# Next layer's modulation weights in a two-layer diffusion backbone: issued without a wait for the pair rows

## The chip, the cores and the metric

The kernel runs on one core of a Trainium2 chip. The metric is the device time of one execution in microseconds (us), as the median of the runs. One core has five engines with instruction streams of their own: TensorE (PE in the profile; its weight loads are PEld), VectorE (DVE), ScalarE (ACT), GpSimd (POOL) and SyncE (SP). They meet only through semaphores. SP and POOL issue transfers, each into a queue of its own, and 16 DMA engines carry out both queues.

## The reference

Two layers (DEPTH = 2) of a hybrid backbone over 384 tokens of 1024 channels, 128 of them context and 256 latent. All data is float32.

```
for l in range(DEPTH):
    mod = silu(c) @ w_mod[l] + b_mod[l]          # 1024 -> 6 * 1024: shift, scale and gate, twice
    u = x * (1 + scale1) + shift1
    x = layer_norm(ALPHA * x + gate1 * token_mixer(u))
    u = x * (1 + scale2) + shift2
    x = layer_norm(ALPHA * x + gate2 * hier_moe(u))
```

`token_mixer` is one input projection (`w_in`), three head groups (pooling, differential attention, convolution) and one output projection (`w_out`). `hier_moe` sends each token to 2 of 32 gated experts and adds their two outputs with their weights:

```
h = silu(t @ w_gate[e]) * (t @ w_up[e])
y = sum over the token's two experts of  w[n, e] * (h @ w_down[e])
```

## The kernel before

Nothing of the weights stays on the core between layers: every weight is loaded from HBM once, in the order in which the layers use it. The big weights go through `ring`, four slots of 24 KB per partition (numbers 0 to 3), and during the experts through a fifth slot (number 4) that lies in `arena`. SP issues all of these loads in one order written out by hand. Before each it waits until the slot's last user is done, so a load that waits also holds back all that stands behind it in SP's stream.

A layer runs through these stages: modulation and input projection (`project`, PE line L828), attention and convolution, output projection (L1010), a first layer norm, the router, then 31 expert chunks `i` = 0 to 30 (between the 20th and the 21st of them some extra chunks for experts with more tokens), then the sum over each token's two experts, a second layer norm (`layer_norm(1)`, PE lines L988, L990 and L997) and, in the first layer, the modulation of the next one.

One chunk is: gather 64 token rows (POOL, L677), transpose them (PE, L1068), multiply by gate and up (PE, L1060), the gate (ACT, L1361, and DVE, L1790), multiply by down (PE, L1075; the last two chunks at L1084), copy out (ACT, L1386), and scatter the result rows to the HBM buffer `y_pairs` (POOL, L682). Chunks 29 and 30 scatter nothing: their results stay in `ystack` on the core. `down_done` counts the chunks whose down product PE has finished.

After chunk 28's scatter has landed, POOL reads `y_pairs` back as three blocks of 128 tokens (L751, into `yk`, 1 MB each, with 8 KB for one partition); each raises its `y_loaded`. These are the pair rows. DVE waits for each block, weighs its two halves and adds them (L1839, L1840), and raises `y_sum`. PE meanwhile multiplies the late chunks' results into place (L1165); then it waits for all three `y_sum` and adds the pair rows (L1174), eight tiles of 384 columns. DVE turns each tile into the residual (L1635, L1642) for the second layer norm.

The next layer's modulation weights come as three loads ("units", `load_mod` at L521, 3, 3 and 2 MB, again 8 KB for one row of one partition). Unit 0 goes into slot 2, whose last chunk is 27, unit 1 into slot 3 (chunk 28) and unit 2 into slot 1 (chunk 29). PE uses them in `mod_product` (L790): k = 0 and 1 inside the second layer norm, the rest after it. Behind the three units SP issues the next layer's `w_in` (L510), once chunk 30 is done.

Of the kernel before, what the change touches and what calls it, by code (L numbers as in the profile page):

```python
# [34 lines left out]
NT = T // P  # L35
# [148 lines left out]
def build(nc, g, consts, lam_dram, u_rows, y_pairs, y_prompt, y_sample, new_k, new_v):  # L184
    with ExitStack() as ctx:
# [3 lines left out]
        def signal(name, per_layer, step=1, credit=0):  # L189
            return Signal(ctx.enter_context(nc.semaphore(name)), per_layer, step, credit)  # L190
# [7 lines left out]
        arena = sb("arena", [P, 2 * XS])  # L198
        pool_sums = sb("pool_sums", [P, 4 * POOL_COLS])
        cst = sb("cst", [P, sum(n for _, n in CONST_COLS)])  # L200
        pool_blk = sb("pool_blk", [P, 2, P])
        conv_pw = sb("conv_pw", [P, 2, CONV])
# [245 lines left out]
        y_loaded = [signal(f"y_pairs_loaded{t}", 1, 16) for t in range(NT)]  # L448
# [8 lines left out]
        def engine_wait(eng):  # L457

            def wait(sig, l, n, alone=False):
                eng.wait_ge(sig.sem, sig.at(l, n))  # L460
                if alone:
                    eng.nop(nofuse=True)
            return wait
# [32 lines left out]
        def _(sp):  # L496
            wait = engine_wait(sp)
# [5 lines left out]
            for l in range(DEPTH):  # L503
# [13 lines left out]
                def load_mod(l_, j, u):  # L517

                    sp.nop(nofuse=True)
                    k0_, k1_ = MOD_K * u, min(KD, MOD_K * (u + 1))  # L520
                    sp.dma_start(mod_w[MOD_SLOTS[j][u]][:, 0:k1_ - k0_, :],  # L521
                                 w_mod[l_:l_ + 1, k0_ * P:k1_ * P, MOD_STEP * j:MOD_STEP * (j + 1)].rearrange(
                                     "o (k p) n -> p (o k) n", p=P)).then_inc(mod_loaded[u].sem, 16)
# [91 lines left out]
                    load_chunk(i)  # L615

                if l + 1 < DEPTH:
                    for t in range(NT):
                        wait(y_loaded[t], l, 1)
                    for u in range(3):  # L620
                        wait(down_done, l, max(i for i in range(NS) if SLOT_OF[i] == MOD_SLOTS[0][u]) + 1)
                        load_mod(l + 1, 0, u)
# [1256 lines left out]
```

## Time and profile before

| | us |
|---|---|
| median of 3 runs | 1119.69 (1119.44 to 1121.03) |
| profiled execution, device time | 1117.82 |
| its span, first to last instruction | 1116.0 |
| PE busy | 929.8 |
| DMA engines, mean rate over the span | 288 GB/s |

All views below are of that one profiled execution; times are us from the start of its span. A row of a timeline is: start, duration, engine, line, operation, destination<-sources, count, and in brackets the engine's idle time before it with what ended it. A row of the chain of work that ended last is: start, duration, engine and line. A row of waits is: who <- whom: us in total, times, longest. A queue's row has its packets, its MB and its share of the 16 DMA engines' time in that stretch: q1 is SP's queue, q0 is POOL's. A row of stretches gives the stretch, its length, busy us of PE, PEld, DVE, ACT and POOL (with instructions), then the granted TensorE clock (1.00 is 2.4 GHz, 0.50 is 1.2 GHz), the DMA engines' busy share and their GB/s. SPq is SP's sequencer as it issues a transfer. A line can be that of a helper.

### The profile page before, as it was taken

The page shows a single profiled execution, that of the slowest core. Times are in us where ns is not written, and L with a number is a line of the kernel's source. Part 1 is how long each engine was busy: PE and PEld are TensorE (multiplying, and loading weights), DVE is VectorE, ACT ScalarE, POOL GpSimd, SP SyncE. Part 2 cuts the span into 40 slices and gives each one's busy share as a digit, 9 for nine tenths or more (in the row PEclk, how much of TensorE's full clock was granted, in tenths as well). Part 3 has the DMA queues.
Part 4 walks back from the last instruction along what each step waited for, and adds up shares of the span by engine and source line. Part 5 has one row for each costly group of instructions (what it writes and reads, how often), then busy time and mean ns, then how long its engine had stood idle before and what let it go on. Part 6 is the DMA issues. An engine that isn't in the chain of part 4 may idle for free.

```text
span 1116.0 us, 13925 instructions
## 1 busy us (share of the span) xinstructions
PE 929.8 (83%) x5252; PEld 549.2 (49%) x5252; DVE 382.8 (34%) x921; ACT 236.9 (21%) x565; POOL 180.0 (16%) x217
## 2 busy tenths in 40 slices
PE   4899988994999877898899989898598896888872
PEld 2456555543555534454455546554355553444441
DVE  0258463255111111113537855126411111111162
ACT  1200166033111100111220036406011110111122
POOL 5000000003223322221020000000333222222100
PEclk8899989996999998999899999999699999989996
DMA  9972163177999999997994226038699999999811
GB/s 359 380 299 77 44 235 154 52 303 288 357 412 415 414 413 413 410 386 278 401 346 182 113 95 268 34 129 345 234 399 413 415 415 383 398 411 411 344 58 57
DMA packets 73136, 321.88 MB, mean 288 GB/s; under 512 B 13150, under 2 KB 17590, under 8 KB 48752
## 3 DMA queue, kind: packets, MB, share of 16 engines
q1 hardware_dynamic: 57824, 294.14, 66.2%
q0 software_dynamic: 15248, 26.87, 6.6%
q8 instruction: 42, 0.69, 0.3%
q14 instruction: 22, 0.18, 0.0%
HBM read 321.46 MB, written 23.59 MB: 309 GB/s over the span
## 4 chain that ended last, share of the span: by engine, by line
PE 62%; DMA 15%; DVE 9%; SPq 8%; ACT 3%; issue 3%; POOLq 0%; POOL 0%; DVEq 0%; ACTq 0%
PE ps L828 13%; PE ps L1060 13%; DMA ring<-in_w_up 9%; PE ps L1010 7%; PE ps L1075 7%; PE ps L831 4%; DMA ring<-in_w_in 3%; SPq L559 3%; SPq L566 2%; SPq L561 2%; PE ps L790 2%; PE ps L997 2%; PE ps L1068 2%; DMA arena<-u_rows,row_idx 1%; PE ps L1084 1%
## 5 line engine op out<-in xcount | busy, mean ns | idle before, releaser
L1060 PE MATMUL ps<-ring,tail 128*64 128x256 f32 x1760 | 204.4, 383 | 12.4 <-DMA ring<-in_w_up 10.6
L1060 PEld LDWEIGHTS ps<-ring,tail 128*64 128x64 f32 x1760 | 143.9, 138 | 84.9 <-issue 24.4
L828 PE MATMUL ps<-uT,ring 128*128 128x384 f32 x448 | 149.7, 492 | 4.1 <-DMA ring<-in_w_in 2.1
L1790 DVE TENSOR_TENSOR arena<-arena,ps 128x128 f32<-128x128 f32 x68 | 19.5, 287 | 364.7 <-ACT arena L1361 364.7
L828 PEld LDWEIGHTS ps<-uT,ring 128*128 128x128 f32 x448 | 85.5, 192 | 60.7 <-issue 3.7
L1075 PE MATMUL ps<-ring,krow 128*64 128x512 f32 x408 | 103.5, 626 | 3.0 <-issue 2.1
L682 POOL DMA_INDIRECT y_pairs<-tail,row_idx x58 | 57.6, 994 | 291.3 <-ACT tail L1386 279.8
L677 POOL DMA_INDIRECT arena<-u_rows,row_idx x66 | 68.9, 1043 | 38.0 <-issue 20.1
L1386 ACT ACTIVATE tail<-ps 128x512 f32<-128x512 f32 x58 | 34.6, 597 | 189.5 <-PE ps L1075 189.5
L1508 DVE SCALAR_TENSOR_TENSOR arena<-arena,dw 128x414 f32<-128x414 f32 x118 | 67.6, 643 | 0.0
L1361 ACT ACTIVATE arena<-ps 128x128 f32<-128x128 f32 x68 | 18.8, 277 | 214.8 <-PE ps L1060 198.6
L1010 PE MATMUL ps<-arena,ring 128*128 128x384 f32 x192 | 62.2, 486 | 0.0
L1068 PE MATMUL ps<-cst,arena 128*128 128x128 f32 x272 | 42.3, 285 | 21.2 <-DMA arena<-u_rows,row_idx 17.4
L1785 DVE COPY tail<-ps 128x512 f32<-128x512 f32 x68 | 46.6, 691 | 37.1 <-PE ps L1068 29.6
L790 PE MATMUL ps<-ring,sT 128*32 128x512 f32 (+1 forms) x512 | 51.7, 544 | 6.2 <-DMA ring<-in_w_mod 6.2
L1122 PE MATMUL ps<-cst,arena 128*128 128x128 f32 x62 | 20.4, 328 | 42.9 <-DVE arena L1790 42.9
L1635 DVE SCALAR_TENSOR_TENSOR uT<-ps,modT,uT 128x128 f32<-128x128 f32 x64 | 23.5, 411 | 81.7 <-PE ps L1010 74.6
L1075 PEld LDWEIGHTS ps<-ring,krow 128*64 128x64 f32 x408 | 29.7, 140 | 41.2 <-issue 41.2
L1010 PEld LDWEIGHTS ps<-arena,ring 128*128 128x128 f32 x192 | 36.5, 190 | 25.4
L1060 PE MATMUL ps<-arena,tail 128*64 128x256 f32 x416 | 48.2, 383 | 0.0
L1068 PEld LDWEIGHTS ps<-cst,arena 128*128 128x128 f32 x272 | 32.2, 146 | 26.4 <-issue 21.0
L1060 PEld LDWEIGHTS ps<-arena,tail 128*64 128x64 f32 x416 | 36.2, 139 | 15.7 <-issue 7.5
(269 smaller groups left out, 980.1 us busy)
## 6 DMA issues: line engine op xcount, KB each, us to landing
ring<-in_w_gate SPq DMA_DIRECT2D x55, 1024.0 KB, 17.8
ring<-in_w_up SPq DMA_DIRECT2D x55, 1024.0 KB, 22.6
ring<-in_w_down SPq DMA_DIRECT2D x55, 1024.0 KB, 23.6
ring<-in_w_mod SPq DMA_DIRECT2D x12, 3072.0 KB, 11.2
arena<-in_w_gate SPq DMA_DIRECT2D x13, 1024.0 KB, 15.8
arena<-in_w_up SPq DMA_DIRECT2D x13, 1024.0 KB, 19.3
arena<-in_w_down SPq DMA_DIRECT2D x13, 1024.0 KB, 18.9
ring<-in_w_mod SPq DMA_DIRECT2D x6, 2048.0 KB, 15.9
```

What stands on the lines that cost most here:

```text
L677: pool.indirect_dma_start(xg[:, b, :], None, u_rows, bass.IndirectOffsetOnAxis(ap=idx, axis=0), bounds_check=2 * T - 1, oob_is_err=False). ...
L682: pool.indirect_dma_start(y_pairs, bass.IndirectOffsetOnAxis(ap=idx, axis=0), rows, None, bounds_check=4 * T - 1, oob_is_err=False).then_i ...
L790: last = mm(ps[32 * g_:32 * (g_ + 1), bank, 0:n], sT[:, 2 * k:2 * k + 32], mod_w[MOD_SLOTS[j][u]][:, row, off + g_ * n:off + (g_ + 1) * n] ...
L828: last = mm(ps[:, n % 4, 0:T], slot[s][:, k, c:c + P], uT[:, k, :], start=(k == 0), stop=(k == KD - 1))
L831: last = mm(ps[:, n % 4, 0:AW], uT[:, k, rows * P:(rows + 1) * P], slot[s][:, k, c:c + AW], start=(k == 0), stop=(k == KD - 1))
L1010: last = mm(ps[:, m % 4, 0:T], wt, mixT[:, k, :], start=(k == 0), stop=(k == KD - 1))
L1060: last = mm(ps[W * half:W * (half + 1), b, 0:2 * P].rearrange("p (j f) -> p j f", j=2), xc[:, b, k, :], gate_up_w[s][:, :, k, half * P:(ha ...
L1068: last = tr(ps[:, 5 + b, c * P:(c + 1) * P], xg[:, buf, c * P:(c + 1) * P], ident)
L1075: last = mm(ps[W * half:W * (half + 1), 3 + b, :], hT[:, b, f * W:(f + 1) * W], down_w[s][:, f, half * 512:(half + 1) * 512], start=(f == ...
L1386: fn(yrow[:, i % 2, :], ps[:, 3 + i % 2, :], ID).then_inc(y_rows.sem, 1)
L1508: conv_own.append(own.add(v.scalar_tensor_tensor(cacc[:, c, :], src, wt, cacc[:, c, :], ALU.mult, ALU.add)))
L1785: v.tensor_copy(xc[:, b].rearrange("p (h j) n -> p j h n", h=2), ps[:, 5 + b, :].rearrange("p (j h n) -> p j h n", j=4, h=2)).then_inc(sig ...
```

## The change

SP no longer waits for the three blocks of pair rows before it issues the three units of the next layer's modulation weights. The wait of each unit for its own slot stays.

```
                 if l + 1 < DEPTH:
-                    for t in range(NT):
-                        wait(y_loaded[t], l, 1)
                     for u in range(3):
                         wait(down_done, l, max(i for i in range(NS) if SLOT_OF[i] == MOD_SLOTS[0][u]) + 1)
                         load_mod(l + 1, 0, u)
```

SP's stream at the end of the first layer, in one piece of the difference: the last expert load (L566), the three units (L521, `ring<-in_w_mod`), and the read of a table that opens the next layer. In brackets stand the semaphores that an instruction waits for; `y_pairs_loaded0` to `2` are `y_loaded`.

```order
 L561 DMA ring<-in_w_up 128x2048
 L566 DMA ring<-in_w_down 128x2x1024 [waits down_done]
-L521 DMA ring<-in_w_mod 128x3x2048 [waits down_done,y_pairs_loaded2,y_pairs_loaded0,y_pairs_loaded1]
-L521 DMA ring<-in_w_mod 128x3x2048 [waits down_done]
+L521 DMA ring<-in_w_mod 128x3x2048 [waits down_done] x2
 L521 DMA ring<-in_w_mod 128x2x2048 [waits down_done]
 L467 TENSOR_LOAD turns_tab
```

No instruction moves within a stream, and the other engines' streams are the same; only the three semaphores ahead of unit 0 are gone.

## Rows read from the trace of the kernel before

**Rows 1.** The profile page: span, and the chain that ended last, by engine.

```profile
span 1116.0 us, 13925 instructions
...
PE 62%; DMA 15%; DVE 9%; SPq 8%; ACT 3%; issue 3%; POOLq 0%; POOL 0%; DVEq 0%; ACTq 0%
```

**Rows 2.** The chain that ended last, end of the first layer.

```profile
522.84 3.63 PE ps L1084 x8
526.49 1.03 ACT arena L1379
527.56 5.43 PE ps L1165 x16
532.99 2.69 PE ps L1174 x24
```

**Rows 3.** SP's waits, 495 to 610 us.

```profile
SPq L460 <- DMA arena<-y_pairs: 28.9, 1, 28.9
```

**Rows 4.** Timeline of SP's issues, 495 to 600 us.

```profile
527.47 1.44 SPq L521 DMA_DIRECT2D ring<-in_w_mod  x3
529.59 32.51 SPq L510 DMA_DIRECT2D ring<-in_w_in  x7
```

**Rows 5.** Timeline of PE, 499 to 550 us.

```profile
500.62 1.94 PE L1075 MATMUL ps<-ring,krow 128*64 128x512 f32 x8
...
507.46 1.94 PE L1075 MATMUL ps<-ring,krow 128*64 128x512 f32 x8
...
517.33 0.59 PE L1084 MATMUL ps<-ring,krow 128*64 128x512 f32 x1
...
532.83 5.52 PE L1174 MATMUL ps<-cst,arena 128*128 128x128 f32 x48
542.06 1.65 PE L988 MATMUL ps<-arena,cst 128*128 128x384 f32 x2 [3.71 <-DVE arena L1642]
```

**Rows 6.** Timeline of PE, 540 to 566 us.

```profile
544.92 3.02 PE L790 MATMUL ps<-ring,sT 128*32 128x512 f32 x16
547.87 5.43 PE L997 MATMUL ps<-arena,cst 128*128 128x384 f32 x16
553.22 5.36 PE L790 MATMUL ps<-ring,sT 128*32 128x512 f32 x48
...
561.97 4.43 PE L828 MATMUL ps<-uT,ring 128*128 128x384 f32 x13 [2.02 <-ACT uT L1211]
```

**Rows 7.** Timeline of POOL, 497 to 521 us.

```profile
510.85 0.97 POOL L682 DMA_INDIRECT y_pairs<-tail,row_idx  x1 [5.82 <-DMA y_pairs<-tail,row_idx]
517.35 1.68 POOL L751 DMA_DIRECT2D arena<-y_pairs  x3 [5.53 <-DMA y_pairs<-tail,row_idx]
```

**Rows 8.** Line L751, 500 to 530 us: issue to landing of its three loads.

```profile
DMA to landing us min/median/max: 5.0/6.9/8.9
```

**Rows 9.** Line L682, 1040 to 1049 us: the last two scatters of the second layer.

```profile
DMA to landing us min/median/max: 6.4/6.5/6.5
```

**Rows 10.** Timeline of DVE, 521 to 545 us.

```profile
527.37 0.75 DVE L1839 TENSOR_SCALAR arena<-arena,r 128x1024 f32<-128x1024 f32 x1 [0.41 <-DMA arena<-y_pairs]
528.15 1.28 DVE L1840 SCALAR_TENSOR_TENSOR arena<-arena,r 128x1024 f32<-128x1024 f32 x1
533.80 1.39 DVE L1635 SCALAR_TENSOR_TENSOR uT<-ps,modT,uT 128x128 f32<-128x128 f32 x4 [4.36 <-PE ps L1174]
```

**Rows 11.** DMA queues, 520 to 526 us: the pair rows alone.

```profile
q0 software_dynamic: 345, 2.56, 101.2%
```

**Rows 12.** DMA queues, 508 to 518 us: the last expert weights.

```profile
q1 hardware_dynamic: 361, 1.73, 42.0%
q0 software_dynamic: 160, 0.07, 2.6%
```

**Rows 13.** DMA queues, 18 to 24 us: both queues full, start of the kernel.

```profile
q1 hardware_dynamic: 208, 1.70, 70.5%
q0 software_dynamic: 215, 0.72, 30.6%
```

**Rows 14.** Stretches of 5 us with clock and DMA, around the second layer norm.

```profile
535.00:540.00 5.00, 3.35 (x30) 3.16 (x29) 4.86 (x13) 0.00 (x0) 0.00 (x0) 1.00 1.00 421
540.00:545.00 5.00, 2.94 (x8) 1.25 (x12) 2.60 (x7) 0.00 (x0) 0.00 (x0) 0.53 1.02 426
```

More of the change, by code:

```diff
@@ L617, in _ @@
                 if l + 1 < DEPTH:
-                    for t in range(NT):
-                        wait(y_loaded[t], l, 1)
                     for u in range(3):
```

## The prediction

> **What bounds the kernel now.** I read the page first, then the chain of work that ended last, then the streams of SP, PE, POOL and DVE around the one place that the change touches, 500 to 562 us. Over the whole span the chain is mostly PE [rows 1], so the question is what PE waits for there. At the end of the first layer the chain runs through PE and ACT without a hole: the down product of chunk 30, ACT's copy, the products of the late chunks (L1165) from 527.56, then the sum of the pair rows (L1174) at 532.99, in the instant at which L1165 ends [rows 2]. So the pair rows are not what PE waits for: DVE finished the third block's sum at 528.15 + 1.28 = 529.43 [rows 10], and 532.99 - 529.43 = **3.56 us** of slack lie between.
>
> Nor are the modulation weights waited for. SP stood 28.9 us before it issued them [rows 3], at 527.47 [rows 4], yet L790 follows its predecessor on PE with no idle time at 544.92 and at 553.22, and the first product of the next layer (L828) waits 2.02 us for ACT's uT and not for `w_in` [rows 6]. SP's 28.9 us are the wait of an engine that nobody is waiting for.
>
> **The change part by part.** *Removed:* the three waits on `y_loaded`. Unit 0 then needs only chunk 27's down product, which ends at 500.62 + 1.94 = 502.56; unit 1 chunk 28's, at 507.46 + 1.94 = 509.40; unit 2 chunk 29's, at 517.33 + 0.59 = 517.92 [rows 5]. Against 527.47 they are issued 25, 18 and 9.5 us earlier. What that gains on the chain is **0**, since no PE instruction of these stages waits for them. `w_in`, next in SP's stream, then waits for chunk 30 alone, 522.84 + 3.63 = 526.47 [rows 2], and goes out 529.59 - 526.47 = 3.1 us earlier: also 0, as L828 waits for ACT.
>
> *Moved:* 8 MB of weights (8.39 million bytes) now meet the pair rows in the DMA engines. Behind chunk 30's expert weights in SP's own queue they delay none of these, so the experts keep their times. POOL's queue is the other one. How much of the 8.39 MB is still to come when the pair rows are issued at 517.35 [rows 7]? From 508 to 518 the engines moved 1.73 + 0.07 = 1.80 MB [rows 12]; at the full rate, 2.56 MB in 6 us = 427 GB/s [rows 11], they could have moved 4.27 MB. The room is 2.5 MB, so at least 5.9 MB of modulation weights are still queued or just being issued: more than the 3.15 MB of the three blocks. The two queues compete for the whole length of the pair rows.
>
> How they share is seen where both were full before: from 18 to 24 us, 208 packets of q1 against 215 of q0 [rows 13]. They take turns packet by packet. Pair rows and modulation rows are both moved as 8 KB pieces, so each queue gets half the bytes. Alone, the pair rows take 3.15 MB / 427 GB/s = 7.4 us; at half the rate 14.7 us. The third block, which landed at 527.37 (where DVE's wait for it ends [rows 10]; 8.9 us after its issue [rows 8]), would land **7.4 us later, at 534.8**. DVE needs 0.75 + 1.28 = 2.03 us for it: `y_sum` at 536.8. PE is through with L1165 at 532.99. The sum: 7.4 - 3.56 = **+3.8 us** of new idle time on PE ahead of L1174. What hid the pair rows before was L1165 and chunk 30; that cover is used up after 3.56 us. Bounds: 0 if the pair rows lost under half of the 7.4 us, +3.8 if they share throughout.
>
> *The scatter ahead of them.* The pair rows are issued when chunk 28's scatter, issued at 510.85, has landed, 6.5 us later [rows 7]. It too now meets weights. At the end of the second layer, with expert weights still coming, the same scatters landed after 6.4 and 6.5 us [rows 9], so I put 0, between 0 and +0.3.
>
> *PE's clock.* A hole of 3.71 us ahead of L988 goes with a granted clock of 0.53 in 540 to 545 us [rows 5, 14], so half the time and more at 1.2 GHz. The new hole is about as long and may bring such a stretch over L1174. Its 48 instructions take 5.52 us, 0.69 us for each of eight tiles; at 1.2 GHz 1.38 us. DVE, which turns the tiles into the residual, starts at 533.80 [rows 10] and lets L988 go after seven of them at 542.06, 1.2 us for each, so it sets the pace and only the first tile is paid in full: **+0.7 us**, from 0 to +1.0. The stretch that now lies on L988 to L790 may move: 16 matmuls of L790 took 3.02 us at 544.92, where 48 took 5.36 us at 553.22 [rows 6], so 16 cost 1.2 us more; with half of L988's 1.65 us and as much for L990, which also lie in it, I bound the gain at 2.8 us. If the stretch fell on L997 instead, up to half of its 5.43 us again, +2.7 us. I take 0 for it, as both are open.
>
> *Queued behind.* All that follows is tied to PE in order: the next layer's `mod_product`, `w_in` of slot 1 (it waits for `mod_rows`), and then the second layer, where each slot is freed by PE. I see no place where 4 us would be won back; a delay here arrives at the end whole.
>
> The sum is 3.8 + 0 + 0.7 = +4.5 us: on the profiled execution 1117.8 + 4.5 = 1122.3, on the median, 1.9 us above it, **1124.2 us** (+0.4%).
>
> **The rivals.** *The pair rows stay hidden.* If the weights got less than half of the engines while the pair rows move, the loss stays under 3.56 us and nothing is left of the change: **1119.7 us**. For it: the slack is real, and the kernel has idle DMA time at 508 to 518. Against it: that room holds 2.5 of 8.4 MB, and turns were equal in rows 13. That unit 0 does not go out early, since something else in SP's stream holds it, would end here too; I see nothing that would. Together 0.15.
>
> *The clock moves to the good side.* The place is L988 to L790. If the stretch at 1.2 GHz falls on the new hole and on L1174, where DVE sets the pace, then L988, L990 and L790 run at 2.4 GHz and win up to 2.8 us: with a hole of next to nothing 1119.7 - 2.8 = **1116.9**. It decides at a hole of 2.8 us, above which it wins nothing; my sum has 3.8. 0.04.
>
> *The weights take more than every second turn.* If q1 drained several 8 KB pieces for each piece of q0, the pair rows would come last: (5.9 + 3.15) MB / 427 GB/s = 21 us from about 518.7, `y_sum` at 542, hole 9 us, **1129 to 1132 us**. Rows 13 speak against it (208 to 215). 0.04. The Trainium skill's page "DMA: Bandwidth & Descriptors" (section "Queues, rings and completion order") has such a rule: an engine goes round the queues, but drains a whole packet, typically 9 to 17 descriptors, before it turns to the next. By that with one piece for one descriptor the time would be this rival's; the trace so far shows equal turns of what it records as packets, and no row here shows how many descriptors one holds.
>
> **How the numbers follow.** Forecast 0.77, hidden 0.15, clock 0.04, unequal turns 0.04. The forecast's own range is from 3.8 - 2.8 = +1.0 (the clock at its best) to 3.8 + 0.3 + 1.0 + 2.7 = +7.8 (scatter and clock at their worst): 1120.7 to 1127.5. Leaving the hidden case out would leave out over 2 in 10, so the range goes down to it: 1119.5 to 1127.5. A measurement can tell about 0.2%, 2.2 us, from no change. Slower by more: all of unequal turns and nearly all of the forecast, 0.79; within: the hidden case and the forecast's low end, 0.17; faster: 0.04.
>
> **What would show it.** In the changed kernel's profile: L521 issued near 502.6, 509.5 and 518 us; in the 8 us after the pair rows' issue, q0 and q1 with about as many packets each; a third landing of some 16 us for L751 where it was 8.9; PE idle some 4 us ahead of L1174, ended by DVE's L1840, where it had no idle time; the granted clock below 1.00 in that stretch; and the second layer shifted as a whole by the same 4 to 5 us. L751's third landing under 12 us would make the sum wrong at its main term; a hole of 4 us with an unchanged total would mean that the loss is won back in the second layer, where I see no place for it.

## The result, and the profile after

| | before, us | changed, us | ratio, 95% interval |
|---|---|---|---|
| first comparison (4 runs each) | 1120.13 | 1129.95 (1128.75 to 1133.26) | 1.0079 (1.0056 to 1.0102) |
| second comparison (26 and 6 runs) | 1121.79 (1117.71 to 1127.56) | 1131.96 (1127.10 to 1133.74) | 1.0083 (1.0054 to 1.0112) |

The change makes the kernel slower by about 0.8%, 9 us (the ratios are estimated from all runs and are not the quotients of the two medians). The forecast was slower by 4.5 us, and the time lies above its range of 1119.5 to 1127.5 us. It lies within the 1129 to 1132 us of the rival of unequal turns; the packets below show that this is chance. The sign and the place were right; the size was half.

The profiled execution of the changed kernel took 1133.26 us, its span is 1131.2 us. Lines of the changed kernel stand two below those of before (L1174 is now L1172, L1165 is L1163, L751 is L749). SP's issues, answering to [rows 4]:

```profile
504.40 15.72 SPq L521 DMA_DIRECT2D ring<-in_w_mod  x3
528.30 19.64 SPq L510 DMA_DIRECT2D ring<-in_w_in  x3
```

The three units go out from 504.40 on (this execution is 1.8 us late at that point, a drift out of the start of the kernel: its product for chunk 27 ends at 504.33 instead of 502.56). The chain of work that ended last no longer runs through PE here, as it did in [rows 2]:

```profile
512.62 7.16 DMA y_pairs<-tail,row_idx
519.85 0.52 issue
520.37 0.86 POOL arena L749 x2
521.49 18.61 DMA arena<-y_pairs
540.12 0.76 DVE arena L1837
540.91 1.29 DVE arena L1838
542.25 2.94 PE ps L1172 x12
```

It goes through the scatter, POOL's issue of the pair rows, 18.61 us for the third block to land (8.9 in [rows 8]), DVE's sum, and only then PE. PE's timeline, answering to [rows 5, 6]:

```profile
529.33 5.43 PE L1163 MATMUL ps<-arena 128*128 128x384 f32 x16 [1.11 <-ACT arena L1377]
542.25 7.07 PE L1172 MATMUL ps<-cst,arena 128*128 128x128 f32 x48 [7.49 <-DVE arena L1838]
552.90 1.65 PE L986 MATMUL ps<-arena,cst 128*128 128x384 f32 x2 [3.58 <-DVE arena L1640]
...
573.29 2.26 PE L826 MATMUL ps<-uT,ring 128*128 128x384 f32 x3 [2.02 <-ACT uT L1209]
```

PE now stands idle for 7.49 us ahead of L1172 until DVE's L1838, where it had no idle time. From the start of L1163 (L1165) to the first L826 (L828) of the second layer PE needs 573.29 - 529.33 = 43.96 us; before it was 561.97 - 527.56 = 34.41 [rows 2, 6]. That is **+9.55 us**: 7.65 from the start of L1163 to that of L1172 (12.92 instead of 5.27), 1.42 from there to L986, 0.48 to L826. The rest of this profile's difference is 1.8 us from the start of the kernel, 3.1 us at L826 itself (below, at the third profile) and 0.8 us in attention.

Why the third block lands so late is told by the packets of the two queues, answering to [rows 11, 13]. From POOL's issue to 524 us, then 524 to 534 us:

```profile
q1 hardware_dynamic: 185, 1.50, 100.0%
```

```profile
q1 hardware_dynamic: 276, 2.13, 51.1%
q0 software_dynamic: 272, 2.10, 50.4%
```

For 3.6 us after its issue no pair row moves at all: 185 weight packets do. From then on the two queues take equal turns, as forecast.

### The profile page after: what moved, and what is told of

Read it like the earlier page. It is cut to its first block, busy times and chain, and to the rows that moved or that the text cites. A ratio compares the mean times of both kernels' runs of the same rounds, so it can differ in the third digit from the quotient of the medians.

```text
span 1131.2 us, 13924 instructions
## 1 busy us (share of the span) xinstructions
PE 933.2 (82%) x5252; PEld 551.5 (49%) x5252; DVE 383.3 (34%) x921; ACT 237.5 (21%) x565; POOL 180.1 (16%) x217
## 4 chain that ended last, share of the span: by engine, by line
PE 60%; DMA 16%; SPq 8%; DVE 8%; ACT 3%; issue 3%; POOL 0%; POOLq 0%; DVEq 0%; ACTq 0%
PE ps L826 13%; PE ps L1058 12%; DMA ring<-in_w_up 9%; PE ps L1008 7%; PE ps L1073 7%; PE ps L829 4%; SPq L559 3%; DMA ring<-in_w_mod 3%; SPq L561 2%; PE ps L788 2%; SPq L566 2%; PE ps L995 2%; DMA y_pairs<-tail,row_idx 2%; DMA arena<-y_pairs 2%; PE ps L1066 2%
## 5 line engine op out<-in xcount | busy, mean ns | idle before, releaser
L826 PE MATMUL ps<-uT,ring 128*128 128x384 f32 x448 | 152.7, 499 | 3.7 <-ACT uT L1209 3.7
L826 PEld LDWEIGHTS ps<-uT,ring 128*128 128x128 f32 x448 | 87.0, 195 | 61.8 <-issue 7.7
L788 PE MATMUL ps<-ring,sT 128*32 128x512 f32 (+1 forms) x512 | 51.4, 542 | 9.1 <-DMA ring<-in_w_mod 9.1
```

The source lines that it names most:

```text
L788: last = mm(ps[32 * g_:32 * (g_ + 1), bank, 0:n], sT[:, 2 * k:2 * k + 32], mod_w[MOD_SLOTS[j][u]][:, row, off + g_ * n:off + (g_ + 1) * n] ...
L826: last = mm(ps[:, n % 4, 0:T], slot[s][:, k, c:c + P], uT[:, k, :], start=(k == 0), stop=(k == KD - 1))
```

## The experiments

All hold the rest of the kernel as it is; r4_small_pieces, r6_pieces_4k and r8_small_rows also raise the semaphore counts that go with more loads. Ratios are to runs of the kernel before on the same chip (median 1121.79 for r1 to r4, 1121.08 for r5 to r8). The third landing counts from the issue of the last load of the pair rows.

| run | what differs from the changed kernel | median, us | ratio, 95% interval | third landing, us | PE idle ahead of the sum, us |
|---|---|---|---|---|---|
| before | the wait on the pair rows | 1120.13 | | 8.9 | 0 |
| changed | | 1129.95 | 1.0079 (1.0056 to 1.0102) | 18.6 | 7.49 |
| r1_again | nothing | 1131.96 | 1.0083 (1.0054 to 1.0112) | 18.7 | 7.65 |
| r2_after_scatter | units wait for the scatters | 1128.72 | 1.0064 (1.0040 to 1.0089) | 18.8 | 6.38 |
| r3_unit0_early | units 1 and 2 wait as before | 1123.32 | 1.0020 (1.0001 to 1.0038) | 15.0 | 3.15 |
| r4_small_pieces | weights in 2 KB pieces | 1121.10 | 0.9997 (0.9973 to 1.0020) | 13.0 | 0.74 |
| r5_again | nothing, one run | 1127.26 | | 18.7 | 7.80 |
| r6_pieces_4k | weights in 4 KB pieces | 1122.87 | 1.0024 (1.0006 to 1.0042) | 14.9 | 2.67 |
| r7_after_block0 | units wait for the first block | 1121.43 | 1.0005 (0.9991 to 1.0018) | 10.1 | 0 |
| r8_small_rows | pair rows in 2 KB pieces | 1138.14 | 1.0157 (1.0129 to 1.0186) | 23.1 | 16.69 |

**The changed kernel again (r1_again).** No edit.

> The changed kernel once more, for its spread and a second profile. The first profile has a hole of 7.5 us on PE ahead of the sum of the pair rows (forecast 3.8), 2.1 us more up to the first L826 of the second layer, and there 3.1 us more in a stretch at 1.2 GHz. Theory A (the hole is made by queues and repeats, the clock stretch over L826 does not): a hole of 7 to 8 us again; a device time near 1129 us if L826's 64 instructions take 20.9 us as before, near 1132 us if they take 23.9 us. Theory B (the size of the hole is itself chance): a hole that differs by over 2 us from 7.5 us.

The hole is 7.65 us and the third landing 18.7 us after its issue: the hole repeats, as in theory A. Its profiled execution took 1132.54 us and has 23.89 us for L826's first 64 instructions; among its runs are also 1127.10 and 1128.35.

**Units behind the scatters (r2_after_scatter).**

```
                 if l + 1 < DEPTH:
+                    for b in range(2):
+                        wait(y_stored[b], l, (PUT + 1 - b) // 2)
                     for u in range(3):
```

> SP waits for the landing of the last scatters, as POOL does, so the three modulation units are issued in the same instant as the pair rows, with nothing of them queued ahead. Theory A (the 3.7 us over the forecast come from weights that were already queued in the DMA engines: 1.25 us on the scatter, 2.3 us before the first pair row moves; the equal turns cost the forecast 7.4 us): scatter back at 6.5 us, third landing of L749 16 to 17 us after its issue (18.6 in the changed kernel), hole near 3.8 us, device time 1124 to 1126 us. Theory B (POOL's transfers start late whenever weights move, whoever was first): third landing 18 to 19 us, hole 6 us, 1127 to 1128 us.

SP and POOL now issue within half a microsecond of each other. SP, POOL and PE in the timeline:

```profile
517.86 1.61 SPq L521 DMA_DIRECT2D ring<-in_w_mod  x3
```

```profile
511.97 0.97 POOL L682 DMA_INDIRECT y_pairs<-tail,row_idx  x1 [5.83 <-DMA y_pairs<-tail,row_idx]
518.37 1.68 POOL L751 DMA_DIRECT2D arena<-y_pairs  x3 [5.43 <-DMA y_pairs<-tail,row_idx]
```

```profile
540.48 7.51 PE L1174 MATMUL ps<-cst,arena 128*128 128x128 f32 x48 [6.38 <-DVE arena L1840]
```

From the scatter's issue to that of the pair rows it is 518.37 - 511.97 = 6.40 us, where the changed kernel has 7.75 (520.37 - 512.62) and the one before 6.50 [rows 7]. So the weights queued ahead cost the scatter 1.3 us, and the hole falls by 1.1 us with it (the ratio of 1.0064 cannot be told from the changed kernel's). But the third block still lands after 18.8 us, and the hole of 6.4 us is theory B's number. My theory A fell on this point: a long line of weights ahead is not needed for the late start. The packets between POOL's issue and 522.3 us are all weights:

```profile
q1 hardware_dynamic: 167, 1.27, 90.6%
```

The half microsecond by which SP is first is enough.

**Unit 0 alone early (r3_unit0_early).**

```
                     for u in range(3):
+                        if u == 1:
+                            for t in range(NT):
+                                wait(y_loaded[t], l, 1)
                         wait(down_done, l, ...)
```

> Only unit 0 goes out early; units 1 and 2 wait for the pair rows as before. Seen over all engines, unit 0's 3.15 MB nearly fit into the 2.5 MB of room that the DMA engines had between 508 and 518 us. Theory A (the room is not spread evenly: the engines that finish the last expert weights late, at 518 us, have all of unit 0 still to move, and a block of pair rows lands with its slowest engine): third landing 14 to 18 us, hole 2 to 7 us, device time 1122 to 1129 us. Theory B (room is room): at most 0.7 MB of unit 0 is left, third landing near 11 us, no hole, 1119.5 to 1121 us.

Unit 0 by itself makes a hole of 3.15 us. It also costs the scatter 1.0 us: from its issue at 513.46 to that of the pair rows at 520.97 it is 7.51 us, where it was 6.50. DVE's three blocks:

```profile
530.34 0.75 DVE L1840 TENSOR_SCALAR arena<-arena,r 128x1024 f32<-128x1024 f32 x1 [4.49 <-DMA arena<-y_pairs]
...
534.66 0.75 DVE L1840 TENSOR_SCALAR arena<-arena,r 128x1024 f32<-128x1024 f32 x1 [2.24 <-DMA arena<-y_pairs]
...
537.12 0.75 DVE L1840 TENSOR_SCALAR arena<-arena,r 128x1024 f32<-128x1024 f32 x1 [0.40 <-DMA arena<-y_pairs]
```

The second block comes 4.3 us after the first, the third 2.5 us after the second, which is the pace of pair rows alone (7.4 us for three). From 522 to 524 us and from 524 to 530 us the packets are:

```profile
q0 software_dynamic: 40, 0.33, 48.6%
q1 hardware_dynamic: 39, 0.32, 37.9%
```

```profile
q0 software_dynamic: 291, 2.16, 85.6%
q1 hardware_dynamic: 47, 0.35, 14.1%
```

With equal turns on all 16 engines the weights would go on at half of the time until they run out on all of them together. Instead they keep on at 14% of it for 6 us. The packets don't name their engine, but this reads as most engines having no weights left after 524 us and a few still having some, and the block lands with these. The numbers are theory A's: the room of 2.5 MB between 508 and 518 us [rows 12] is not shared evenly by the engines, and an average over 16 of them hides it. Pair rows also begin to move 1.3 us after their issue (13 packets of q0 from 522.2 to 523.2, with the issue at 520.97), as in the kernel before; the weights took 38.9% of the engines' time between that issue and 522.2. So POOL's transfers are not late in themselves. They start late where the engines are full of weights.

**Weights in 2 KB pieces (r4_small_pieces).**

```
+                    n = MOD_STEP // pieces
+                    for c in range(pieces):
+                        sp.dma_start(mod_w[...][:, 0:k1_ - k0_, c * n:(c + 1) * n], w_mod[... + c * n ...])
...
-                        load_mod(l + 1, 0, u)
+                        load_mod(l + 1, 0, u, 4)
```

> The three units go out as early as in the changed kernel, but each as four loads of 512 columns, so in pieces of 2 KB instead of 8 KB. Theory A (turns are taken piece by piece, whatever its size, and the start of the pair rows waits for a number of pieces): an 8 KB pair row of 309 ns now alternates with 88 ns, so the pair rows take 9.5 us instead of 14.7 us, and start some 0.6 us instead of 2.3 us late: third landing 11.5 to 13 us, hole 0 to 1 us, 1119.5 to 1121.5 us. Theory B (the queues share by bytes or time): third landing 16 to 19 us and a hole of 4 to 7.5 us, 1125 to 1130 us.

The units go out as early as in the changed kernel, the total is that of the kernel before, and the hole is 0.74 us. The packets from 524 to 530 us:

```profile
q0 software_dynamic: 265, 1.93, 78.8%
q1 hardware_dynamic: 257, 0.52, 22.7%
```

Still one packet each, 265 to 257, but the pair rows now take 1.93 MB against 0.52. The late start was mis-sized here: pair rows are absent from their issue at 519.68 to 522.1 (2.4 us, against 1.3 us in the kernel before and 3.6 in the changed one), so it is 1.1 us and more, and not the quarter of 2.3 us that I had expected.

This run also answers whether the early units cost anything outside the pair rows. To within the interval, about 0.25% either way, they do not: with the pair rows less disturbed and a hole of 0.74 us, the loss is gone.

**The changed kernel a third time (r5_again).** No edit.

> The changed kernel a third time, for a profile. Two profiles had L826 of the second layer with a stretch at 1.2 GHz (23.9 us for its first 64 instructions instead of 20.9) and device times of 1133.3 and 1132.5 us; other runs of it took 1127 to 1129 us. Theory A (that stretch is the difference between the two): a device time near 1129 us comes with 20.9 us for L826, one near 1132 us with 23.9 us; the hole ahead of L1172 is 7.5 us in either. Theory B (the hole itself differs): a fast run with a hole of 4 to 5 us.

One run, with a device time of 1127.26 us and a hole of 7.80 us, so theory B falls. PE's timeline:

```profile
543.50 8.58 PE L1172 MATMUL ps<-cst,arena 128*128 128x128 f32 x48 [7.80 <-DVE arena L1838]
554.23 0.91 PE L986 MATMUL ps<-arena,cst 128*128 128x384 f32 x2 [2.15 <-DVE arena L1640]
...
571.69 20.88 PE L826 MATMUL ps<-uT,ring 128*128 128x384 f32 x64 [2.02 <-ACT uT L1209]
```

L826 takes 20.88 us as before, where the first two profiles have 23.93 and 23.89. The granted clock at that place, first the profile of the result, then this one:

```profile
573.00:578.00 5.00, 4.71 (x8) 2.62 (x9) 4.62 (x15) 4.26 (x9) 4.26 (x8) 0.50 1.04 416
```

```profile
571.00:576.00 5.00, 4.31 (x14) 2.62 (x15) 4.66 (x13) 4.66 (x10) 3.86 (x7) 1.00 1.03 414
```

In one the engine is at 1.2 GHz, in the other at 2.4. PE had the same gap of 2.02 us ahead of L826 in both. Here also L986 and L788 ran at 2.4 GHz (0.91 us for two where the first profile has 1.65), so from L986 to L826 it took 17.46 us instead of 20.39. The clock thus makes about 6 us of difference between two profiled executions with nearly the same hole, of which theory A had the half at L826. That is about the spread of all runs, 1127 to 1134 us; the others have no profile.

**Weights in 4 KB pieces (r6_pieces_4k).** The edit of r4_small_pieces, with 2 for 4.

> The units as early as in the changed kernel, each as two loads of 1024 columns, in pieces of 4 KB, between the 8 KB of the changed kernel and the 2 KB of the former run. Theory A (turns piece by piece): a pair row of 309 ns alternates with 159 ns, 11.2 us for all instead of 14.7 and 9.5; with a late start of 1.3 to 2 us the third landing is 14 to 15 us after its issue, the hole 1.5 to 3 us, the ratio to before 1.002 to 1.005. Theory B (2 KB pieces were harmless for another reason, such as their longer issue on SP): a hole under 0.8 us or one as long as in the changed kernel.

Third landing 14.9 us, hole 2.67 us, ratio 1.0024: all three within theory A. Equal turns again from 524 to 530 us:

```profile
q0 software_dynamic: 220, 1.67, 66.9%
q1 hardware_dynamic: 216, 0.86, 35.6%
```

The late start is as long as with 8 KB pieces: no pair row moves from the issue at 518.83 to 522.6, 3.8 us. That is 2.5 us more than in the kernel before, where theory A had put 1.3 to 2.

**Units behind the first block (r7_after_block0).**

```
+                    wait(y_loaded[0], l, 1)
                     for u in range(3):
```

> SP waits for the first block of the pair rows alone, then issues the units as their slots allow. Theory A (what counts is who is in the engines first, and how long the two are there together): at that landing some 2 of 3 blocks are through, the rest alternates, third landing at most 12 us after its issue, no hole, ratio 1.000. Theory B (pair rows are slowed whenever weights are issued near them): third landing 14 us or more and a hole of 2 us or more.

Third landing 10.1 us, no idle time on PE, ratio 1.0005. Pair rows that are in the engines first lose 1.2 us to the weights that come 5 us behind them, and 3.56 us of slack cover it.

**Pair rows in 2 KB pieces (r8_small_rows).** The reverse of r4_small_pieces, to double the suspected cost.

```
-                    pool.dma_start(yk[:, t, :], ...)
+                    for r_ in range(4):
+                        pool.dma_start(yk[:, t, r_ * 512:(r_ + 1) * 512], ...)
```

> The changed kernel with the pair rows in pieces of 2 KB (four loads for each block) and the weights in 8 KB as before: the reverse of the run with small weight pieces. Theory A (turns piece by piece): 96 small pair rows for each engine stand against 8 KB weight rows first and 2 KB rows of w_in later, 19 us for the first half and 8 us for the second, third landing some 27 to 30 us after the first issue, hole 15 to 18 us, device time 1138 to 1143 us. Theory B (shares by bytes or time): a hole of 8 to 9.5 us, 1129 to 1134 us.

```profile
550.46 7.56 PE L1173 MATMUL ps<-cst,arena 128*128 128x128 f32 x48 [16.69 <-DVE arena L1839]
```

```profile
q1 hardware_dynamic: 387, 2.80, 68.7%
q0 software_dynamic: 385, 1.27, 32.4%
```

The hole is 16.69 us. From 524 to 534 us the queues move 387 and 385 packets, and the pair rows get under a third of the bytes. A share by bytes or by time would have given 8 to 9.5 us by the estimate of theory B. The landing's 23.1 us count from the last of twelve issues, which POOL spreads over 6.5 us; from the first it is 29.0, within theory A's 27 to 30.

But what took turns was not what theory A had added up. The packets by size in the same 10 us:

```profile
DMA packets 772, 4.07 MB, mean 407 GB/s; under 512 B 98, under 2 KB 98, under 8 KB 438
```

The mean packet of q0 is 1.27 MB / 385 = 3.3 KB, more than a piece. Over the whole transfer the trace has 768 packets of 4096 bytes, two of the 2 KB pieces in each, and 16 packets of 4 bytes for each of the twelve loads. The equal counts include the small ones. So an engine had on average 48 packets of pair rows and not 96, and that the hole came out within 15 to 18 us is in part luck. The run shows equal turns by packet; it does not show them piece by piece.

## Why the prediction was wrong in size

**What bounds, and what the change gains.** Right. The 3.56 us of slack, nothing gained on PE, no instruction of PE waiting for the modulation weights: r4_small_pieces and r7_after_block0 have the units early and are as fast as the kernel before, not faster.

**The turns.** Right in packets, and shown at three sizes of weight pieces and with small pair rows. The Trainium skill's page "DMA: Bandwidth & Descriptors" (section "Queues, rings and completion order") says that an engine goes round its queues packet by packet. The trace agrees for what it records as packets, 276 to 272, 265 to 257 and 387 to 385. The rival of unequal turns is refuted by these counts, though its 1129 to 1132 us were met: its 9 us of hole came from pair rows that move last, and the measured 7.5 us do not. How many pieces one packet holds is another matter: with 8 KB rows it is one, in r8_small_rows it is two.

**The step that failed: what the pair rows and the scatter lose before the first turn.** The working put the whole loss into the 7.4 us of shared turns and let them start as soon after the issue as before (1.3 us). Measured, the third landing is 18.6 - 8.9 = 9.7 us later: 7.4 of turns, and 2.3 of a late start (3.6 against 1.3) that the sum did not have. The scatter, put at 0 to 0.3 us by [rows 9], lost 1.25 us (7.75 against 6.50). The sum then comes out: 1.25 + 2.3 + 7.4 - 3.56 = 7.4 us, where the profile has 7.49 and the forecast 3.8.

Both could be read in the trace of before. The 6.5 us of [rows 7] run from the scatter's issue to the issue of the pair rows, the 6.4 and 6.5 us of [rows 9] from issue to landing, so the working set two different measures side by side. From issue to landing chunk 28's scatter took 5.9 us, while the weights took 38.9% of the engines' time from its issue to 512.4 us. The first scatter of [rows 9] was issued at 1039.68 with the engines full of expert weights, and nothing of it moves for 4.1 us. Before, 510.85 to 512.4 us, then 512.4 to 513.4, then 1039.68 to 1043.8:

```profile
q1 hardware_dynamic: 34, 0.25, 38.9%
...
y_pairs<-tail,row_idx POOLq DMA_INDIRECT x1, 5.9
```

```profile
q0 software_dynamic: 50, 0.00, 2.5%
```

```profile
q1 hardware_dynamic: 321, 1.72, 102.5%
...
y_pairs<-tail,row_idx POOLq DMA_INDIRECT x1, 6.4
```

So [rows 9] did show a loss, of 0.5 to 0.6 us; in the changed kernel it is 1.25 us (7.16 in the chain above, against 5.9). Why it is larger there stays open.

The late start comes with engines that are busy with weights (r3_unit0_early), needs no long queue ahead (r2_after_scatter), and falls away when the pair rows are there first (r7_after_block0). What sets its length stays open. Beyond the 1.3 us of before it is 2.3 us or more with 8 KB pieces, 2.5 with 4 KB and 1.1 with 2 KB. With the 309, 159 and 88 ns for a piece that the expectations use, that is by estimate about 7, 16 and 13 pieces for each engine, or 60, 64 and 25 KB: neither one number of pieces, nor one amount of data, nor one time fits all three.

**The average over engines.** The 2.5 MB of room were an average. The forecast came to full sharing all the same, since 5.9 MB were left; but with unit 0 alone the same working would have said that nearly nothing is left, and r3_unit0_early measures a hole of 3.15 us.

**The clock.** L1172 to L986 took 1.42 us more where I had put 0.7, at most 1.0 (L1172's first 12 products took 2.94 us, where 24 took 2.69 [rows 2]). The rival of the good side did happen, in r5_again, at the place and nearly with the price that I gave (L986 to L826 2.4 us shorter than the 19.91 us of before, against 2.8), but beside a hole of 7.8 us. What I had not seen is a stretch at 1.2 GHz over L826, 3.1 us, in two of the three profiles. It is part of the spread from 1127 to 1134 us. The hole of 7.5 us alone would have left the forecast's +4.5 too low, by 3 us, but within its range (1119.7 + 7.5 = 1127.2). In the profiled execution the clock's 1.42, 0.48 and 3.1 us come on top; r5_again, where it gave back 2.4 us, took 1127.26 us.

**The second layer.** Right: from L826 on the delay arrives whole. From the first L826 to the end of the span it is 1125.4 - 571.69 = 553.7 us in r5_again, where it was 1116.0 - 561.97 = 554.0 before.

## What to carry to other kernels

A wait of an idle queue engine can be worth its time: it kept a load that nobody needed yet out of the way of one that had 3.56 us to spare. Before bringing a bulk load forward, look at what the other queue moves in that stretch: count its packets and not its bytes, add a late start on top of the shared turns, and take the slowest engine and not the mean. Where both must move at once, put the urgent transfer in first, or cut the other one into smaller pieces.

## What the runs showed of the hardware

- Two queues that both have work on the DMA engines move equal numbers of packets, whatever the sizes: 276 to 272 at 8 KB each, 257 of 2 KB to 265 of 8 KB, 216 of 4 KB to 220 of 8 KB, and 387, most of 8 KB, to 385, most of 4 KB (small packets counted). The size of a packet is thus a priority.
- A packet is not always one piece: POOL's 2 KB rows moved two to a packet of 4 KB (r8_small_rows, mean 3.3 KB), SP's 2 KB rows one to a packet (r4_small_pieces, 0.52 MB / 257 = 2.0 KB).
- A transfer of POOL's that comes to engines full of SP's 4 or 8 KB pieces starts late: the pair rows 3.6 to 3.9 us after their issue instead of 1.3, the scatter at 1039.68 us of before more than 4.1 us instead of 1.55. With 2 KB pieces the pair rows start after 2.4 us.
- With the same work and the same gap of 2.02 us on PE ahead of it, L826 has a stretch at 1.2 GHz in one execution and runs at 2.4 GHz in another, 3.1 us apart. A hole of 7.80 us gave 7.0 us of delay at L826 in one profile (41.43 us from L1163 to L826 against 34.41), one of 7.49 us gave 9.55 us in another.
